# Sums on top of the scores in their bank, and two heads' scores from stacked operands

## The reference, cut to what matters

```python
z = jnp.einsum('bhqd,bhkd->bhqk', qblk, kh) * scale
strict = kpos[None, :] < qp[:, None]
log_beta = jax.nn.log_sigmoid(z)
log_keep = jnp.where(strict, jax.nn.log_sigmoid(-z), 0.0)
between = lax.cumsum(log_keep, axis=..., reverse=True) - log_keep
w = jnp.where(strict, jnp.exp(log_beta + between), 0.0)
out = jnp.einsum('bhqk,bhkd->bhqd', w, vh)
```

## Time and profile before

| | us |
|---|---|
| median of the runs | 2635.23 |
| profiled execution, its own time | 2635.47 |
| its span, first to last instruction | 2633.7 |
| TensorE matmul busy | 2621.3 |
| DVE busy | 1790.2 |
| ACT busy | 1310.9 |
| POOL busy | 608.1 |

### The profile page before, as it was taken

How to read it: one execution, slowest core, us unless ns; L and a number is a source line. 1 busy time by engine, 2 the same in 40 slices (tenths; PEclk the granted TensorE clock), 3 DMA queues, 4 the chain that set the end, 5 groups by cost and what they waited for, 6 DMA issues and landing times.

```text
span 2633.7 us, 33670 instructions
## 1 busy us (share of the span) xinstructions
PE 2621.3 (100%) x13168; PEld 2224.4 (84%) x13168; DVE 1790.2 (68%) x2771; ACT 1310.9 (50%) x2086; POOL 608.1 (23%) x674
## 2 busy tenths in 40 slices
PE   9999999999999999999999999999999999999999
PEld 7888889899888888888888888888888888888887
DVE  7656576666666646666475768876777568876677
ACT  5323353334346636533225677754445677754445
POOL 0000111011026627510002744420100544420100
PEclk9999999999999999999999999999999999999999
DMA  4233266466322232232222421355651321355650
GB/s 168 96 97 99 89 167 157 132 157 160 111 66 65 69 89 60 73 103 96 96 96 74 124 85 49 110 149 154 176 152 43 106 71 49 122 151 148 176 144 32
DMA packets 92111, 287.13 MB, mean 109 GB/s; under 512 B 10928, under 2 KB 13488, under 8 KB 91952
## 3 DMA queue, kind: packets, MB, share of 16 engines
q1 hardware_dynamic: 80784, 257.18, 30.2%
q0 software_dynamic: 11168, 27.79, 6.4%
HBM read 274.45 MB, written 2.10 MB: 105 GB/s over the span
## 4 chain that ended last, share of the span: by engine, by line
PE 92%; DVE 5%; ACT 2%; issue 0%; POOL 0%; DMA 0%; SPq 0%; DVEq 0%; ACTq 0%
PE ps L490 26%; PE ps L491 26%; PE ps L492 26%; PE ps L497 3%; PE ps L496 3%; PE ps L495 3%; DVE ptl L2117 1%; PE ps L715 1%; PE ps L569 0%; DVE s L2746 0%; DVE s L2743 0%; PE ps L776 0%; PE ps L775 0%; ACT s L1534 0%; ACT s L1745 0%
## 5 line engine op out<-in xcount | busy, mean ns | idle before, releaser
L490 PE MATMUL ps<-xh,wh 128*128 128x512 f32 (+1 forms) x1808 | 696.7, 385 | 0.5 <-POOL wl L3170 0.5
L491 PE MATMUL ps<-xl,wh 128*128 128x512 f32 (+1 forms) x1808 | 692.6, 383 | 0.0
L492 PE MATMUL ps<-xh,wl 128*128 128x512 f32 (+1 forms) x1808 | 692.4, 383 | 0.0
L1283 ACT ACTIVATE wh<-raw 128x1024 fp32r<-128x1024 f32 (+3 forms) x387 | 389.7, 1008 | 481.1 <-PE ps L492 410.7
L2109 DVE TENSOR_TENSOR wl<-raw,wh 128x1024 fp32r<-128x1024 f32 (+2 forms) x277 | 331.2, 1196 | 110.8 <-ACT wh L1283 110.3
L490 PEld LDWEIGHTS ps<-xh,wh 128*128 128x128 f32 x1808 | 340.1, 188 | 67.6 <-POOL wl L3170 1.4
L492 PEld LDWEIGHTS ps<-xh,wl 128*128 128x128 f32 x1808 | 339.9, 188 | 66.6
L491 PEld LDWEIGHTS ps<-xl,wh 128*128 128x128 f32 x1808 | 340.1, 188 | 65.0 <-issue 1.0
L3170 POOL TENSOR_TENSOR wl<-raw,wh 128x256 fp32r<-128x256 f32 x392 | 302.5, 805 | 388.5 <-ACT wh L1283 362.1
L490 PE MATMUL ps<-yh,wh 128*128 128x512 f32 x640 | 251.4, 393 | 0.7 <-ACT s L1534 0.7
L491 PE MATMUL ps<-yl,wh 128*128 128x512 f32 x640 | 249.4, 390 | 0.0
(11 more groups left out here) (370 smaller groups left out, 5224.9 us busy)
## 6 DMA issues: line engine op xcount, KB each, us to landing
raw<-in_ff SPq DMA_DIRECT2D x64, 512.0 KB, 5.9
a<-in_ff2t SPq DMA_DIRECT2D x64, 512.0 KB, 7.5
raw<-in_pool_in SPq DMA_DIRECT2D x62, 512.0 KB, 3.4
raw<-in_conv_in SPq DMA_DIRECT2D x50, 512.0 KB, 4.0
raw<-in_pool_out SPq DMA_DIRECT2D x32, 512.0 KB, 3.4
raw<-in_qk SPq DMA_DIRECT2D x32, 512.0 KB, 3.6
sw<-in_conv_in SPq DMA_DIRECT2D x42, 256.0 KB, 3.9
raw<-in_pool_grp SPq DMA_DIRECT2D x16, 512.0 KB, 3.5
```

Of the source, the lines that this page charges most:

```text
L490: pe.do.matmul(o, lh, rh_, start=start, stop=False)
L491: pe.do.matmul(o, lh, rl_, start=False, stop=False)
L492: return pe.do.matmul(o, ll, rh_, start=False, stop=stop)
L1283: act.do.activation(h[:, 0:ncol], r[:, 0:ncol], ACT.Copy).then_inc(*mark("whi", ("whi", k)))
```

## The change

The sums of `sb_between` are no longer written into a bank of their own: they are added onto the scores, which stay in their bank. For that the high half of keep is taken with a minus sign (`high` with scale -1, `low_scaled`), and the triangle holds the diagonal too, so that the bank ends as z - keep - sums, the logarithm of the weight. ACT's exponent then reads the bank itself and is what frees it. `SL`, the first pass of `soft` and DVE's `between` are gone. In `weights_of` ACT takes the three exponents first and the three high halves after them.

Heads 3 and 5 take their scores from two stacked tiles (key high over key low, query high twice) for the first four matmuls, and from the plain 64-row halves (key high by query low) for the other four. The tiles are filled by four DMAs per head on SP's queue.

```diff
+                def sb_scores_short(h):
+                    k_hl, q_hh = SHORT[h]
+                    q_l, k_h = sqk(h // 2)[1:3]
+                    rr = slice(64 * (h % 2), 64 * (h % 2) + 64)
+                    pe.wait_ge(*at("stackq", l, h))
+                    pe.wait_ge(*at("stackk", l, h))
+                    pe.wait_ge(*at("ones"))
+                    for n, (kbs, k0, width) in enumerate(GR):
+                        use(sb_banks[n], ("ss", l, h, kbs[0]))
+                    for pas in range(2):
+                        for kbs, k0, width in GR:
+                            b = ps("ss", l, h, kbs[0])
+                            for kb in kbs:
+                                o = b[:, KOFF[kb] - k0:KOFF[kb] - k0 + 512 - 128 * kb]
+                                kc, qc = slice(kb * 128, kb * 128 + 128), slice(kb * 128, 512)
+                                if pas == 0:
+                                    pe.do.matmul(o, k_hl[:, kc], q_hh[:, qc], start=kb == kbs[0], stop=False)
+                                else:
+                                    pe.do.matmul(o, k_h[rr, kc], q_l[rr, qc], start=False, stop=False)
...
                 def sb_between(h):
...
-                        b = use(sb_banks[n], ("sb", l, h, kbs[0]))
-                        pe.do.matmul(b[:, 0:width], trir[:, :], SBH[:, k0:k0 + width], start=True, stop=False)
+                        b = ps("ss", l, h, kbs[0])
+                        pe.do.matmul(b[:, 0:width], trir[:, :], SBH[:, k0:k0 + width], start=False, stop=False,
+                                     skip_group_check=True)
...
-                sb_scores(3)
+                sb_scores_short(3)
...
-                sb_scores(5)
+                sb_scores_short(5)
...
-                        high(SBH[:, k0:k0 + n], SA[:, k0:k0 + n], ("kept", l, h, kbs[0]), ("kph", l, h, kbs[0]))
+                        high(SBH[:, k0:k0 + n], SA[:, k0:k0 + n], ("kept", l, h, kbs[0]), ("kph", l, h, kbs[0]), -1.0)
...
                 def weights_of(h):
-                    act.wait_ge(*at("mm", "sb", l, h, 0))
                     for kbs, k0, n in GR:
-                        act.wait_ge(*at("logw", l, h, kbs[0]))
-                        act.do.activation(SA[:, k0:k0 + n], SA[:, k0:k0 + n], ACT.Exp).then_inc(
-                            *mark("act", ("wexp", l, h, kbs[0])))
+                        act.wait_ge(*at("mm", "sb", l, h, kbs[0]))
+                        act.do.activation(SA[:, k0:k0 + n], ps("ss", l, h, kbs[0])[:, 0:n], ACT.Exp).then_inc(
+                            *mark("act", ("wexp", l, h, kbs[0]), ("psfree", "ss", l, h, kbs[0])))
+                    for kbs, k0, n in GR:
                         high(SBH[:, k0:k0 + n], SA[:, k0:k0 + n], ("wexp", l, h, kbs[0]), ("bph", l, h, kbs[0]))
...
-                        dve.do.scalar_tensor_tensor(SL[:, k0:k0 + n], src, 0.0, a, ALU.min, ALU.subtract).then_inc(
-                            *mark("dve"))
-                        dve.wait_ge(*mine())
                         dve.do.scalar_tensor_tensor(a, src, 0.0, a, ALU.max, ALU.add).then_inc(
-                            *mark("dve", ("kept", l, h, kbs[0]), ("psfree", "ss", l, h, kbs[0])))
+                            *mark("dve", ("kept", l, h, kbs[0])))
...
-                def between(h):
...
-                        dve.do.tensor_tensor(SA[:, k0:k0 + n], SL[:, k0:k0 + n], ps("sb", l, h, kbs[0])[:, 0:n],
-                                             ALU.subtract).then_inc(
...
+            def stack_short(l, h):
+                rr = slice(64 * (h % 2), 64 * (h % 2) + 64)
+                q_h, _, k_h, k_l = sqk(h // 2)
+                k_hl, q_hh = SHORT[h]
+                sp.wait_ge(*at("pl", l, "sk", h // 2))
+                sp.do.dma_start(f(k_hl[0:64, :]), f(k_h[rr, :])).then_inc(*mark(f"stackk{h}", by=16))
+                sp.do.dma_start(f(k_hl[64:128, :]), f(k_l[rr, :])).then_inc(*mark(f"stackk{h}", ("stackk", l, h), by=16))
+                sp.wait_ge(*at("pl", l, "sq", h // 2))
+                sp.do.dma_start(f(q_hh[0:64, :]), f(q_h[rr, :])).then_inc(*mark(f"stackq{h}", by=16))
+                sp.do.dma_start(f(q_hh[64:128, :]), f(q_h[rr, :])).then_inc(*mark(f"stackq{h}", ("stackq", l, h), by=16))
...
                 stack_k(l, 2)
+                stack_short(l, 3)
+                weights(unit["wo", l, 0, 0])
+                stack_short(l, 5)
                 weights(unit["wo", l, 1, 2])
```

More of the change, by code:

```diff
@@ L376, in program @@
         m_chunk = const[:, C_CHUNK:C_CHUNK + 128]
-        m_before, m_after = OB[:, 0:128], OB[:, 128:256]
+        m_before, m_from = OB[:, 0:128], OB[:, 128:256]
         eps = const[:, C_EPS:C_EPS + 1]
@@ L406, in program @@
         STACKS = {1: G[12:15], 2: G[15:18], 7: XH[0:3]}
-        SA, SL, SBH, SBL = SETS[0]
+        SHORT = {3: (YH[1], YL[1]), 5: (YH[2], YL[2])}
+        SA, _, SBH, SBL = SETS[0]
         def v_block(which, part, tb, is_low):
@@ L980, in sb_between @@
                 def sb_between(h):
-                    for n, (kbs, k0, width) in enumerate(GR):
+                    for kbs, k0, width in GR:
                         for jb in range(kbs[0], 4):
                             pe.wait_ge(*at("kpl", l, h, {0: 0, 1: 1, 2: 2, 3: 2}[jb]))
-                        b = use(sb_banks[n], ("sb", l, h, kbs[0]))
-                        pe.do.matmul(b[:, 0:width], trir[:, :], SBH[:, k0:k0 + width], start=True, stop=False)
-                        pe.do.matmul(b[:, 0:width], trir[:, :], SBL[:, k0:k0 + width], start=False, stop=False)
+                        b = ps("ss", l, h, kbs[0])
+                        pe.do.matmul(b[:, 0:width], trir[:, :], SBH[:, k0:k0 + width], start=False, stop=False,
+                                     skip_group_check=True)
+                        pe.do.matmul(b[:, 0:width], trir[:, :], SBL[:, k0:k0 + width], start=False, stop=False,
+                                     skip_group_check=True)
                         for jb in range(kbs[0] + 1, 4):
@@ L989, in sb_between @@
                             cc = slice(KOFF[jb], KOFF[jb] + 512 - 128 * jb)
-                            pe.do.matmul(o, onesr[:, :], SBH[:, cc], start=False, stop=False)
-                            mm = pe.do.matmul(o, onesr[:, :], SBL[:, cc], start=False, stop=jb == 3)
+                            pe.do.matmul(o, onesr[:, :], SBH[:, cc], start=False, stop=False, skip_group_check=True)
+                            mm = pe.do.matmul(o, onesr[:, :], SBL[:, cc], start=False, stop=jb == 3,
+                                              skip_group_check=True)
                         mm.then_inc(*mark("group", ("mm", "sb", l, h, kbs[0])))
@@ L2198, in load @@
                 dve.do.tensor_copy(onesr[:, :], ones)
-                dve.do.tensor_copy(trir[:, :], m_after)
+                dve.do.tensor_copy(trir[:, :], m_from)
                 dve.do.tensor_scalar(hidden[:, :], m_before, 1.0, -NEG, ALU.subtract, ALU.mult).then_inc(
@@ L2742, in soft @@
                         dve.wait_ge(*at("soft", l, h, kbs[0]))
-                        dve.do.scalar_tensor_tensor(SL[:, k0:k0 + n], src, 0.0, a, ALU.min, ALU.subtract).then_inc(
-                            *mark("dve"))
-                        dve.wait_ge(*mine())
                         dve.do.scalar_tensor_tensor(a, src, 0.0, a, ALU.max, ALU.add).then_inc(
-                            *mark("dve", ("kept", l, h, kbs[0]), ("psfree", "ss", l, h, kbs[0])))
+                            *mark("dve", ("kept", l, h, kbs[0])))
                 def keep(h):
                     for kbs, k0, n in GR:
-                        low(SBL[:, k0:k0 + n], SA[:, k0:k0 + n], SBH[:, k0:k0 + n], ("kph", l, h, kbs[0]),
-                            ("kpl", l, h, kbs[0]))
-                def between(h):
-                    for kbs, k0, n in GR:
-                        dve.wait_ge(*at("mm", "sb", l, h, kbs[0]))
-                        dve.do.tensor_tensor(SA[:, k0:k0 + n], SL[:, k0:k0 + n], ps("sb", l, h, kbs[0])[:, 0:n],
-                                             ALU.subtract).then_inc(
-                            *mark("dve", ("logw", l, h, kbs[0]), ("psfree", "sb", l, h, kbs[0])))
+                        low_scaled(SBL[:, k0:k0 + n], SA[:, k0:k0 + n], SBH[:, k0:k0 + n], -1.0,
+                                   ("kph", l, h, kbs[0]), ("kpl", l, h, kbs[0]))
                 def weights_of(h):
@@ L2855, in second_layer @@
                 rot("dq", 0)
-                between(0)
                 turned("dk", 0)
@@ L2867, in second_layer @@
                 project("sk", 1)
-                between(1)
                 df_max(0, 32)
@@ L2885, in second_layer @@
                 df_max(1, 34)
-                between(2)
                 v_low(1, 0)
@@ L2907, in second_layer @@
                 plain("sq", 2)
-                between(3)
                 weights_of(3)
@@ L2919, in second_layer @@
                 project("sq", 3)
-                between(4)
                 df_turn(2)
```

(5 more changed lines are left out.)

2 lines of the change are left out of this document (1 added, 1 removed).

## The result

The changed kernel takes 2640.66 us (median of 19 runs, 2637.78 to 2642.06) against 2635.27 for the kernel before (19 runs, 2634.68 to 2637.15): ratio 1.002, interval 1.0013 to 1.0026. It is slower by 5.4 us. The forecast was 2636.0 with a range up to 2640.5. The granted clock of its runs is 0.996 to 0.998; those of the kernel before have 0.999 to 1.000. Such a figure is a mean over the run: behind the last matmul the clock goes to 0.50 in every profile (before: last matmul at 2627.39, 0.67 in the window of 2630 to 2634), which costs nothing.

What follows compares the result with a forecast made beforehand. TensorE was taken to bound the kernel, 92% of the chain. Per layer +1.43 us at head 6 less 1.03 at head 7 gave +0.4, +0.8 for two: forecast 2636.0 us against the median 2635.23, range 2630.5 to 2640.5.

Steps and rivals of the forecast that it cites:

- rival B: Head 6's bank: none of DVE's saving arrives, scores start at 1655.0; +2.5 us a layer, 2640.2; chance 0.16.
- Head 3's start: Short scores wait for all three banks, freed by ACT's exponents: 1568.55 instead of 1567.61, +0.9, net +0.3 us.
- head 4's lateness: Scores wait for head 3's first exponent on ACT: +1.15 us, together with head 3 +1.5.
- head 6's scores: They wait for head 5's first exponent on ACT, start at 1653.25 instead of 1651.82: TensorE +1.43 us there.
- Rival A: DVE's freed time reaches ACT in full: -1.25 us a layer, 2632.7, or 2630.4 without head 4's wait; chance 0.20.
- Head 7: Wait before its values product, behind DVE's low halves, goes as `between` is dropped: -1.03 us a layer.
- The net without the clock: Sum of all terms: +0.4 us per layer, +0.8 over the two layers.
- The shorter scores: Heads 3 and 5 with fewer matmuls: 0.6 and 0.5 us less in each layer.
- The stacks and DMA: Eight more SBUF copies per layer on SP's queue: some 20 us of cover, nothing on the path.

Runs made afterwards that it cites:

- the first profile: Profiled run of the changed kernel, nothing else altered: 2637.78 us, clock 0.998.
- the second: Changed kernel once more, unaltered, for a second profile: profiled run 2640.26 us; median of 11 runs 2640.26, ratio 1.0018.
- the 1.09 us above: Head 6's stop in the changed kernel without the short scores of heads 3 and 5: median 2638.12 us, ratio 1.0009.
- the 2.02: Second-layer stop in the kernel before with only a wait on head 5's exponents put ahead of head 6's scores: median 2640.93 us, ratio 1.0023.

## Why the prediction was wrong

The step that failed is the sum. It put each wait in at its own length ("+0.3 + 1.15, then what is set at head 6: +1.43 in all, - 1.03 = +0.4. Two layers: +0.8") and gave TensorE's stops no price beyond that. The runs showed a second price: the clock falls to half after some of the stops, 3.45 us in the first profile and 6.9 in the second, and with the stops filled the kernel takes 2634.77. The bound on the slow side, 2640.5, came from rival B, another mechanism that did not occur; that 2640.66 lies so close to it is luck.

- *The waits: right in place, cause and size.* Head 3's start was given as 1568.55 and came at 1568.66; head 4's lateness as 1.5 (1.93: the run was 0.20 late before, head 3's scores took 1.64 and not 1.53, and the bank came free some 0.2 later); head 6's scores as 1653.25 (1653.48), from ACT's exponent at 1652.7 (1652.92). Rival A did not occur: the wait at head 6 is whole. Nor did B: 1653.48 is far from its 1655.0.
- *Head 7: right.* The wait is gone. TensorE is there 0.18 early and not 0.4 late: between head 6 and head 7 it made up another 0.8, and where was not followed further.
- *The net without the clock: +0.8 forecast, -0.3 measured* (all three waits filled, of which the fill costs some 0.6), -1.0 by the clock column of the first profile. So the sum of the waits was too high by 1 to 2 us, and most of that is the 0.8 a layer made up on the way to head 7.
- *The shorter scores: 2.2 forecast, 1.97 to 2.15 measured* with nothing behind them.
- *The stacks and DMA: right.* No wait of TensorE on a transfer appears.
- *What the profile of before could have told:* its clock is 1.00, with two stops of about 0.9 a kernel at head 7. The prediction had the change bring four longer ones, of 1.1 at head 4 and over 1 at head 6 in each layer, and did not ask whether the clock outlasts these. It was a bound to be put in as unknown, upwards.

Not settled: what decides whether a given stop is followed by a fall, and how long that lasts (1.7 to 3.5 us lost each). The length of the stop alone does not: a fall followed the 1.09 us above and none the 2.02. No run tried stops of graded lengths.

## What to carry to other kernels

A stop of TensorE that a change adds has two prices, its length and the clock after it, and the second can be the larger; look at the granted clock behind each new wait, since the busy column reads full there. When a wait is moved to another engine, go through that engine's queue as well: here ACT stood idle ahead of work that was not ready, with the wanted exponents ready behind it, and putting them first, with one block of TensorE's moved as well, turned a loss of 5.4 us into a gain of 8.7. Where the order can't be changed, matmuls for nothing in the gap held the clock.

## What was not expected of the hardware

- After stops of 1.1 to 2.0 us in a stage that else keeps TensorE busy, the granted clock fell to 0.50 in some cases and not in others: the seven profiles with such stops in the attention stages hold 20 of them, and a fall follows 11. After the stops of 0.78 to 0.89 us at heads 3 and 7 no profile here shows one.
- Matmuls that do nothing useful, 26 a layer, made the changed kernel 5.9 us faster (2640.66 to 2634.77) and narrowed its runs from 4.3 us to 0.5.
- The row of a wait can name the wrong releaser: a wait put in on ACT's exponent was listed under DVE, which had ended an instruction close to the same time.
